# First projection in row halves with turned tiles between its chunks, and earlier requests for small inputs and for the second expert tile's weights

## What is computed

```python
n = rms_norm(h, norm1_g[l])                 # h is x, 1024 x 1024
proj = n @ w_in[l]
(q_att, c_kv, q_idx, k_idx, w_idx, r_q, r_k, r_v, r_gate, g_att, g_ret) = jnp.split(proj, points, axis=-1)
...                                         # sparse indexed attention, retention, gated merge, h = h + mixed @ w_out
n2 = rms_norm(h, norm2_g[l])
h = h + hierarchical_moe(n2, ...)           # top-1 group, top-2 of 16 experts, SwiGLU
```

## Time and profile before

| | us |
|---|---|
| median of the three runs | 1532.45 |
| the profiled execution | 1532.13 |
| its span | 1530.3 |
| PE busy in the span | 1447.9 |
| DVE busy | 1089.7 |
| ACT busy | 769.0 |
| POOL busy | 570.6 |
| mean granted TensorE clock | 0.973 |

### The profile page before, as it was taken

One profiled execution on the slowest core, in us unless ns is written; L12 is line 12 of the kernel. 1 busy time (PEld: TensorE's weight loads), 2 busy tenths in 40 slices (PEclk: granted clock), 3 DMA queues, 4 the chain that ended last, 5 costly groups with the idle time before them and its releaser, 6 DMA issues.

```text
span 1530.3 us, 19995 instructions
## 1 busy us (share of the span) xinstructions
PE 1447.9 (95%) x7190; PEld 1203.0 (79%) x7190; DVE 1089.7 (71%) x1518; ACT 769.0 (50%) x1270; POOL 570.6 (37%) x418
## 2 busy tenths in 40 slices
PE   5999999999999998899999999999999489999995
PEld 5987888987889887677667788888887478888884
DVE  4328999999999965776648943236533689999994
ACT  5237323236422526766533442223335378888884
POOL 2310221463424276100135543332232156775655
PEclk9998999999999998999999999999999599999998
DMA  5210121113221034111155334445325888899995
GB/s 193 63 35 1 35 49 42 42 35 110 79 53 42 22 115 167 56 56 28 42 192 192 98 125 143 148 147 174 148 83 185 286 278 253 272 241 354 271 292 75
DMA packets 93937, 199.91 MB, mean 131 GB/s; under 512 B 11664, under 2 KB 33424, under 8 KB 91536
## 3 DMA queue, kind: packets, MB, share of 16 engines
q1 hardware_dynamic: 76560, 158.01, 30.7%
q0 software_dynamic: 13392, 32.51, 9.7%
q10 hardware_dynamic: 3888, 8.13, 1.4%
HBM read 206.22 MB, written 39.58 MB: 161 GB/s over the span
## 4 chain that ended last, share of the span: by engine, by line
PE 74%; DMA 10%; DVE 6%; ACT 3%; issue 3%; POOL 2%; ACTq 0%; SPq 0%; DVEq 0%; POOLq 0%
PE ps L782 21%; PE ps L783 21%; PE ps L784 21%; DMA out<-e_y,dest 8%; PE ps L1011 4%; PE ps L1001 2%; DVE dist L1735 1%; DMA w_raw<-in_w_in 1%; PE ps L1144 1%; PE ps L949 1%; DMA xin<-in_x 1%; POOL out L2319 1%; PE ps L962 1%; DVE f_sum L1846 1%; DMA e_raw<-in_w_up 1%
## 5 line engine op out<-in xcount | busy, mean ns | idle before, releaser
L2178 POOL TENSOR_TENSOR w_lo<-w_raw,w_hi 128x512 fp32r<-128x512 f32 (+1 forms) x184 | 254.7, 1389 | 599.8 <-ACT w_hi L1219 523.4
L1219 ACT CAST w_hi<-w_raw 128x512 fp32r<-128x512 f32 (+1 forms) x184 | 111.8, 614 | 402.9 <-PE ps L784 352.2
L782 PE MATMUL ps<-w_hi,n_hi 128*128 128x512 f32 (+2 forms) x704 | 243.7, 346 | 1.8 <-ACT ro L1378 1.6
L784 PE MATMUL ps<-w_hi,n_lo 128*128 128x512 f32 (+2 forms) x704 | 242.0, 344 | 0.0
L783 PE MATMUL ps<-w_lo,n_hi 128*128 128x512 f32 (+2 forms) x704 | 241.9, 344 | 0.0
L2116 DVE TENSOR_TENSOR e_lo<-e_raw,e_hi 128x2048 fp32r<-128x2048 f32 x93 | 213.2, 2296 | 29.3 <-ACT e_hi L1610 28.8
L1610 ACT CAST e_hi<-e_raw 128x2048 fp32r<-128x2048 f32 x93 | 177.8, 1914 | 40.5 <-DMA e_raw<-in_w_up 24.1
L2319 POOL DMA_INDIRECT out<-e_y,dest x62 | 142.5, 2299 | 99.6 <-DMA out<-e_y,dest 72.2
L1774 DVE MAX8 small<-dist 128x8 f32<-128x384 f32 (+5 forms) x192 | 171.8, 895 | 6.6
L782 PE MATMUL ps<-n_hi,w_hi 128*128 128x512 f32 x416 | 164.3, 395 | 6.6 <-POOL w_lo L2178 2.6
L1775 DVE MATCH_REPLACE8 dist<-small,dist 128x384 f32<-128x384 f32 (+5 forms) x192 | 168.1, 875 | 0.0
(11 more groups left out here) (277 smaller groups left out, 2858.1 us busy)
## 6 DMA issues: line engine op xcount, KB each, us to landing
e_raw<-in_w_gate SPq DMA_DIRECT2D x64, 512.0 KB
e_raw<-in_w_up SPq DMA_DIRECT2D x64, 512.0 KB
e_raw<-in_w_down SPq DMA_DIRECT2D x32, 1024.0 KB
w_raw<-in_w_in SPq DMA_DIRECT2D x120, 256.0 KB, 2.7
a_raw<-att_dram SPq DMA_DIRECT2D x16, 512.0 KB, 3.4
a_raw<-ret_dram SPq DMA_DIRECT2D x16, 512.0 KB, 3.3
w_raw<-in_w_out SPq DMA_DIRECT2D x24, 256.0 KB, 3.4
w_raw<-in_w_in SPq DMA_DIRECT2D x40, 128.0 KB, 2.3
```

The costliest lines, as they stand in the source:

```text
L782: mm(out, a[0], b[0], start=first, stop=False, skip_group_check=skip)
L784: return mm(out, a[1], b[0], start=False, stop=last, skip_group_check=skip)
L1219: nc.scalar.copy(w_hi[c % NH][:, :width], split_from(c)[:, :width]).then_inc(hi_ready, 1)
L2178: G.tensor_tensor(w_lo[c % NH][:, :width], split_from(c)[:, :width], w_hi[c % NH][:, :width].bitcast(F32), ALU.subtract).then_inc(lo_ready, 1)
```

## The change

The first projection's first four row tiles are taken ahead of the others. PE turns the first four row tiles one by one as they are scaled; it then takes chunks 0 and 1 for row tiles 0 to 3, turns half of the other four tiles, takes chunk 2, turns the rest, takes chunk 3, takes chunks 0 to 3 for row tiles 4 to 7, and chunks 4 to 7 for all. The second half is turned into banks 4 to 7 alone. `hi(3)` goes ahead of `turned_hi(1)`, and `hi(0)` stands between the two halves of `turned_hi(0)`. 1/rms and the scaling go tile by tile, and the last row tile is squared on DVE. The identity and the gains are loaded behind the second row tile, the rest of `cst` and `w_up` behind the first four chunks; whoever reads them waits for `rest_in`. The residual's x tiles reuse the semaphores of the first x loads. SP no longer waits ahead of tile 1's expert weights.

```diff
-        for half in range(2):
-            for k in range(KT):
-                bk.use(("xT", half, k), k)
-        use_block("kv")
+        for k in range(KT):
+            bk.use(("xT", 0, k), k)
+        for b in range(4):
+            bk.use(("kv", b), b)
+        for k in range(KT):
+            bk.use(("xT", 1, k), 4 + k % 4)
+        for b in range(4, 8):
+            bk.use(("kv", b), b)
@@ SP
-                if t == 3:
-                    sp.dma_start(cst[:], w["cst"]).then_inc(const_in, 16)
+                if t == 1:
+                    sp.dma_start(cst[:, K_ID:K_REL], w["cst"][:, K_ID:K_REL]).then_inc(const_in, 16)
                     sp.dma_start(gains[:, 0:NGAIN], w["gains"]).then_inc(const_in, 16)
-            for j in range(2):
-                sp.dma_start(w_up[:, j, :], w["w_kv_up"][j * P:(j + 1) * P, :]).then_inc(up_in, 16)
             for c in range(ga + 4):
                 load_chunk(c)
+                if c == NR - 1:
+                    sp.dma_start(cst[:, K_REL:], w["cst"][:, K_REL:]).then_inc(rest_in, 16)
+                    for j in range(2):
+                        sp.dma_start(w_up[:, j, :], w["w_kv_up"][j * P:(j + 1) * P, :]).then_inc(up_in, 16)
...
-                if i.n == 1:
-                    sp.wait_ge(ex_in[1], 16)
@@ PE
-            for half in range(2):
-                pe.wait_ge(xn_done, 4 * (half + 1))
+            for t in range(4):
+                pe.wait_ge(xn_done, t + 1)
                 for k in range(KT):
-                    bk.wait_free(pe, ("xT", half, k))
+                    last = turn_x(0, k, t)
+                    if t == 3:
+                        bk.filled(last, ("xT", 0, k))
+            def turn_second(ks):
+                pe.wait_ge(xn_done, NT)
+                for k in ks:
+                    bk.wait_free(pe, ("xT", 1, k))
                     for t in range(4):
...
-            gemm("kv")
+            def kv_rows(k, tiles):
+                c = number["kv"] * KT + k
+                pe.wait_ge(lo_ready, c + 1)
+                for b in tiles:
+                    if k == 0:
+                        bk.wait_free(pe, ("kv", b))
+                    t = slice(b * P, (b + 1) * P)
+                    last = three(bank(("kv", b), KVW), (n_hi[:, k, t], n_lo[:, k, t]),
+                                 (w_hi[c % NH][:, :KVW], w_lo[c % NH][:, :KVW]), k == 0, k == KT - 1)
...
+            kv_rows(0, range(4))
+            kv_rows(1, range(4))
+            turn_second(range(0, 4))
+            kv_rows(2, range(4))
+            turn_second(range(4, KT))
+            kv_rows(3, range(4))
+            for k in range(4):
+                kv_rows(k, range(4, 8))
+            for k in range(4, KT):
+                kv_rows(k, range(8))
...
+            pe.wait_ge(rest_in, 16)        # ahead of the index products; ACT, DVE and POOL wait for it too
@@ ACT
-            square_x(range(NT))
+            square_x(SQ_ACT)               # SQ_ACT = range(NT - 1)
             act.wait_ge(const_in, 16 * 2)
-            turned_hi(0)
-            for c in range(NH - 1):
+            turned_hi(0, range(0, 4))
+            hi(0)
+            turned_hi(0, range(4, KT))
+            for c in range(1, NH):
                 hi(c)
             turned_hi(1)
@@ DVE
-            for pair in range(NT // 2):
-                dve.wait_ge(rstd1, pair + 1)
-                for t in range(2 * pair, 2 * pair + 2):
-                    V.tensor_scalar(xin[:, t, :], xin[:, t, :], small[:, 8 + t:9 + t], None, ALU.mult).then_inc(xn_done, 1)
+            def square_x(t):
+                dve.wait_ge(x_in[t], 16)
+                V.tensor_tensor_reduce(out=junk_v[:], in0=xin[:, t, :], in1=xin[:, t, :], scale=1.0, scalar=0.0,
+                                       op0=ALU.mult, op1=ALU.add, accum_out=small[:, t:t + 1]).then_inc(sq_dve, 1)
+            for t in range(5):
+                norm_x(t)                  # waits for rstd1 >= t + 1, then the same scaling of one tile
+            square_x(NT - 1)
             dve.wait_ge(const_in, 16 * 2)
+            turned_lo(0, range(0, 4))
+            for t in range(5, NT):
+                norm_x(t)
+            turned_lo(0, range(4, KT))
+            turned_lo(1)
...
-            turned_lo(0)
-            turned_lo(1)
@@ POOL
-            for pair in range(NT // 2):
-                pool.wait_ge(sq_done, 2 * (pair + 1))
-                rstd(small[:, 8 + 2 * pair:10 + 2 * pair], small[:, 2 * pair:2 * pair + 2], 2, D, (rstd1, 1))
+            for t in range(NT):
+                if t in SQ_ACT:
+                    pool.wait_ge(sq_done, SQ_ACT.index(t) + 1)
+                else:
+                    pool.wait_ge(sq_dve, 1)
+                rstd(small[:, 8 + t:9 + t], small[:, t:t + 1], 1, D, (rstd1, 1))
```

More of the change, by code:

```diff
@@ L265, in program @@
         junk = r1t("junk", [P, 2, D], 15488)
+        junk_v = r1t("junk_v", [P, D], 15488 + 2 * D)
         rqT = [r1t(f"rqT{i}", [P, S], i * S) for i in range(2)]
@@ L364, in program @@
         n2_dram = scratch["n2"]
-        const_in, up_in = sem("const_in"), sem("up_in")
+        const_in, rest_in, up_in = sem("const_in"), sem("rest_in"), sem("up_in")
         x_in = [sem(f"x_in{t}") for t in range(NT)]
@@ L373, in program @@
         s_dve, s_act, s_pool = sem("dve_seq"), sem("act_seq"), sem("pool_seq")
+        sq_dve = sem("sq_dve")
         sq_done, rstd1, xn_done, nhi_done = sem("sq_done"), sem("rstd1"), sem("xn_done"), sem("nhi_done")
@@ L393, in program @@
         mixed, mix_hi, mix_lo = sem("mixed"), sem("mix_hi"), sem("mix_lo")
-        xres_in, h_stored = [sem(f"xres_in{t}") for t in range(NT)], sem("h_stored")
+        h_stored = sem("h_stored")
         rt_in, h_half_sq, h_sq, h_rstd, n2_done, n2_stored = (sem(n) for n in ("rt_in", "h_half_sq", "h_sq", "h_rstd", "n2_done", "n2_stored"))
@@ L554, in program @@
             {"block": use_block, "phase1": use_phase1, "phase2": use_phase2, "turn": use_turn, "first": use_first}[what](n)
+        SQ_ACT = range(NT - 1)
         STEPS = NT * HA
@@ L716, in _ @@
                     for t in range(2 * k - 8, 2 * k - 6):
-                        sp.dma_start(xres[:, t, :], w["x"][t * P:(t + 1) * P, :]).then_inc(xres_in[t], 16)
+                        sp.dma_start(xres[:, t, :], w["x"][t * P:(t + 1) * P, :]).then_inc(x_in[t], 16)
             def load_weights(b, j, e, **new):
@@ L859, in _, with turn_x @@
             pe.wait_ge(const_in, 16 * 2)
-            for half in range(2):
-                pe.wait_ge(xn_done, 4 * (half + 1))
+            def turn_x(half, k, t):
+                return tr(bank(("xT", half, k))[:, t * P:(t + 1) * P], xin[:, 4 * half + t, k * P:(k + 1) * P], ident)
+            for t in range(4):
+                pe.wait_ge(xn_done, t + 1)
                 for k in range(KT):
-                    bk.wait_free(pe, ("xT", half, k))
-                    for t in range(4):
-                        last = tr(bank(("xT", half, k))[:, t * P:(t + 1) * P],
-                                  xin[:, 4 * half + t, k * P:(k + 1) * P], ident)
-                    bk.filled(last, ("xT", half, k))
-            gemm("kv")
+                    last = turn_x(0, k, t)
[5 more added lines that the diff above has]
+                    bk.wait_free(pe, ("xT", 1, k))
+                    for t in range(4):
+                        last = turn_x(1, k, t)
+                    bk.filled(last, ("xT", 1, k))
+            def kv_rows(k, tiles):
[7 more added lines that the diff above has]
+                                 (w_hi[c % NH][:, :KVW], w_lo[c % NH][:, :KVW]), k == 0, k == KT - 1)
+                    if k == KT - 1:
+                        bk.filled(last, ("kv", b))
+                    elif b == 7:
+                        last.then_inc(chunk_used, 1)
+            kv_rows(0, range(4))
[8 more added lines that the diff above has]
+                kv_rows(k, range(8))
             gemm("qi")
@@ L1223, in square_x, with turned_hi @@
                     act.wait_ge(x_in[t], 16)
[L1224 to L1229, removed]
+                    n = SQ_ACT.index(t)
+                    if n >= 2:
+                        act.wait_ge(sq_done, n - 1)
+                    A(junk[:, n % 2, :], xin[:, t, :], ACT.Square, accum_out=small[:, t:t + 1]).then_inc(sq_done, 1)
+            def turned_hi(half, ks=range(KT)):
+                for k in ks:
                     name = ("xT", half, k)
@@ L1243, in ahead @@
                     hi(number[name] * KT + k + NH - 1)
-            ahead("kv")
+            for c in range(NH, KT + NH - 1):
+                hi(c)
             for t in range(NT):
@@ L1254, in _ @@
             act.wait_ge(gains_done, 1)
+            act.wait_ge(rest_in, 16)
             for j in range(2):
@@ L1673, in _, with turned_lo @@
             V = nc.vector
-            def turned_lo(half):
-                for k in range(KT):
+            def turned_lo(half, ks=range(KT)):
+                for k in ks:
                     name = ("xT", half, k)
```

(21 more changed lines are left out.)

## The result

| | median us | lowest to highest, runs | ratio to before, 95% interval | profiled, us | its span |
|---|---|---|---|---|---|
| before | 1531.53 | 1529.22 to 1533.86, 6 | | 1532.13 | 1530.3 |
| changed | 1522.38 | 1519.90 to 1524.33, 6 | 0.9939 [0.9925, 0.9952] | 1520.5 | 1518.7 |
| changed, measured again (e10 below) | 1522.18 | 1520.53 to 1524.75, 6 | 0.9940 [0.9927, 0.9953] | 1524.75 | 1523.0 |

The kernel became 0.6% faster: 9.2 us between the medians, 9.3 [7.4, 11.5] by the ratio. 1524.0 had been forecast, in a range of 1519.5 to 1530.5.

A forecast was written before the change was run, and what follows sets the result against it. PE was taken to bound the kernel, with 74% of the chain of waits (DMA 10%). 1532.13 - 4.2 (head) - 4.2 (expert stage) = 1523.7, the median 0.3 higher: 1524.0 us, range 1519.5 to 1530.5.

The forecast's parts named there:

- Loads: Head: identity and gains ahead add 0.19 us; third row tile lands at 7.86, the last at 14.35 instead of 17.38.
- The square on DVE: Head: DVE squares the last row tile from 14.35, taken as 1.2 us, between 1.06 and 2.3.
- rival B: Head: the low clock lasts 10 us and DVE's square costs 2.3 us; 1527.2 us in total; chance 14%.
- Start and clock: Head: PE starts the projection at 18.2, low clock for 5.1 us, block "qi" at 53.4 instead of 57.63, gaining 4.2 us.
- Rival D: Head: PE never gets the high clock while turns and chunks alternate, so the kernel is slower, 1536.3 us; chance 4%.
- The value of the clock: Head: each further us of low clock costs 0.46 us; no low stretch at all would gain 6.5 us.
- Issue and landing of tile 1's weights: Expert stage: tile 1's loads start at 1208.5, the first part lands at 1218.7; PE's 4.6 us gap falls to 1.
- The expert term: Expert stage: the next result is turned at 1235.8 instead of 1239.97, gaining 4.2 us; bounds 2.7 and 5.2.
- Rival A: Expert stage: early weights only fill the queue or scatters absorb the gain, so it gives nothing; 1528.2 us; chance 17%.
- Gathers: Expert stage: earlier weights touch only the end of tile 0's gather, nothing charged; by the queue rule 4.0, not 4.2.
- Rival C: Expert stage: all 3 MB of weights go ahead of tile 0's rows, 2.6 us lost; 1530.8; 10% with both parts lost.
- The end: Last chain: the scatter-adds have caught up with PE, so the kernel's end moves with PE.

The follow-up runs named there:

- e10: The changed kernel itself without an edit, measured again: 1522.18 us, 0.9940.
- e1: The changed kernel with the wait ahead of tile 1's expert weights put back, so the head's part alone: 1524.00 us, 0.9950.
- e2: The kernel before with only the wait ahead of tile 1's expert weights taken out: 1526.39 us, 0.9967.
- e4: The changed kernel with the old order of loads and tile 1's wait put back, so the new order of work alone: 1527.87 us, 0.9975.
- e6: The changed kernel with the last row tile squared on ACT, as before the change, instead of DVE: 1523.74 us, 0.9953.
- e7: The changed kernel with PE repeating the first half's last transpose 28 times to shorten its idle stretch ahead of the projection: 1523.29 us, 0.9950.
- e3: The kernel before with the new loads, tile-by-tile 1/rms and scaling and DVE's square, but the old PE and ACT order and the wait: 1527.36 us, 0.9971.
- e5: The changed kernel with DVE squaring the last row tile behind its first four low parts instead of in front: 1525.02 us, 0.9957.
- e8: The changed kernel with chunk 0 loaded behind the fourth row tile and the work of ACT, POOL, DVE and PE reordered: 1520.43 us, 0.9933.
- e9: As e8, but POOL computes 1/rms of row tiles 6 and 7 as one pair: 1520.27 us, 0.9929.

## Why the prediction was right, point by point

- **Loads.** Third tile 7.86 and last 14.35 predicted; 7.89 and 14.31 measured. The distance between them, the rate, holds elsewhere too (8.49 and 14.91 in e1, 8.45 and 14.89 in e10). The exact hit of the first was a favourable draw: in the eight other profiles with these loads the third tile stands at 7.95 to 8.49, and the mean of the nine is 8.21. With the old loads it is 7.67, 7.38 (e2) and 7.40 (e4), mean 7.48. So the term for identity and gains ahead of the third tile, 0.19, is 0.7 between the means.
- **The square on DVE.** 1.2 was taken, out of 1.06 to 2.3; it is 1.23. The dear square of rival B is out, and e6 shows that the square is on the path when it stands in front of ACT's evictions.
- **Start and clock.** Start at 18.2 predicted, 18.03 measured, 18.44 in e1 and 18.61 in e10. Low for 5.1 us from there predicted; windows of 0.1 us put the return of the clock at 22.4 (4.4 us), 24.1 in e1 and 24.4 in e10 (5.7 and 5.8). In all three the granted clock was low for 6.8 us; it fell at 15.6, 17.3 and 17.6, inside the idle stretch. So 5.1 was a fair mean, and a single draw is 0.6 to 0.7 off. 0.27 a matmul instead of 0.28. Block "qi" at 53.4 predicted; 52.59, 53.56 (e1) and 53.46 (e10), mean 53.2, measured, against 57.63 and 57.23 (e2) for the old head, mean 57.4: 4.2 us, the predicted term. Rival D, a clock that never comes back, is out: it is 1.00 from 25 on in all three.
- **Small slips.** The old head's turns took 6.13 / 32 = 0.192 and 6.58 / 32 = 0.206 us each, not 0.205 in both halves, and low for 10 us gives 4.9 x 0.46 = 2.3 less, so 2.0 and not 2.1. Neither changes the forecast.
- **The value of the clock.** "Each further us of low clock costs 0.46" is the step that does not hold below the forecast: e7 took the low stretch away, and 0.86 us of it came back as a wait for POOL. It made the bound of 6.5 too high and left the sum alone.
- **Issue and landing of tile 1's weights.** Its first part 14.3 us behind the token predicted (1218.7 - 1204.43), 13.5 measured, 13.5 to 14.9 over the eight executions. Gap of PE 1 predicted, 0.93 measured, up to 1.42 in the eight.
- **The expert term.** 4.2 predicted, 4.8 between the two profiles (35.54 - 30.73), 3.5 between the means of four executions with the wait and eight without (33.76 - 30.30). The mechanism was right; that the size fits is in part luck. The reference was read off one execution whose gap, 4.67 us, is the longest of the four that keep the wait, and whose second turn is 1.8 us above their mean (35.54 against 33.76). The forecast turn, 1235.8 - 1204.43 = 31.4, is 1.1 above the mean of the eight: tile 2's weights were put on ACT 26.6 us behind the token and came at 24.4 to 25.8. The two errors nearly cancel. e2's median says 4.6 by itself. Rival A (early weights only fill the queue) is out: e2 alone gives 0.9967 [0.9956, 0.9979].
- **Gathers.** No delay was charged. Tile 0's rows reach PE 5.7 to 6.0 us behind the token in the four profiles with the wait and 5.6 to 6.2 in the eight without, in the mean 5.84 and 5.81. Rival C is out. The Trainium skill's rule of turns between queue rows (page "DMA: Bandwidth & Descriptors", section "Queues, rings and completion order"), by which tile 0's gather should lose a few tenths, is neither shown nor excluded by this: the spread is as large, and PE had no wait for a later tile's rows.
- **The end.** The last turn of a result moved from 1510.29 to 1498.52 and the last scatter from 1520.18 to 1508.53, 11.8 and 11.65: the end moves with PE, as said. The last scatter starts 9.9 to 10.1 us behind the last turn in eleven of the twelve profiles; in e10 it is 12.5, so 2.5 us of that slow execution were lost behind PE.
- **The sum.** 4.2 + 3.5 = 7.7 by positions, 9.3 [7.4, 11.5] by the ratio. Of the 11.6 between the first two profiles, 2.0 is the stretch with the wait at 793 us; in the other executions that wait is 0.28 to 1.37 or absent, as in e2, e3 and both of the changed kernel. The medians' 1.5 us beyond 7.7 lie inside the interval. The stretch from block "qi" to the token took 1144.8 to 1147.4 us over the twelve profiles, and both old heads (1146.8 and 1145.6) lie inside that: a spread wider than the missing 1.5 us. But e1, the head alone, is 6.9 [4.7, 10.7] us faster, where the positions count 4.2. Whether the head gains something that they do not show, the runs leave open.

## What to carry to other kernels

Before moving one operation, list what the engines have in program order behind whoever waits for its result: e5 freed DVE and blocked POOL. Count a stall's removal only up to the next engine that is late there, as e7 and e8 showed, where 0.86 and 1.43 us came back as other waits. And size a DMA wait from several executions, for the one that was profiled may hold the longest gap.

## What had not been expected of the hardware

The clock's fall was not a matter of the idle stretch's length alone. Behind 3.11 us of idle (e4) PE stayed at 2.4 GHz, and behind 1.84 us (e9) it went to 1.2 GHz. The windows of e4, of e9 and of the kernel before, the clock in the last column but two:

```profile
18.00:21.00 3.00, 0.12 (x1) 0.12 (x2) 3.00 (x7) 3.00 (x7) 2.34 (x4) 1.00 0.28 76
21.00:24.00 3.00, 2.20 (x13) 1.93 (x14) 3.00 (x5) 2.28 (x6) 1.37 (x2) 1.00 0.23 56
```

```profile
15.00:19.00 4.00, 3.75 (x16) 3.21 (x17) 4.00 (x7) 4.00 (x9) 2.84 (x3) 0.75 1.04 395
19.00:22.00 3.00, 3.00 (x17) 3.00 (x17) 3.00 (x5) 1.29 (x3) 2.09 (x4) 0.77 0.68 184
```

```profile
19.00:21.00 2.00, 0.00 (x0) 0.00 (x0) 1.39 (x3) 2.00 (x5) 0.58 (x1) 1.00 0.03 9
21.00:22.00 1.00, 0.00 (x0) 0.00 (x0) 0.97 (x5) 1.00 (x3) 0.00 (x0) 0.60 0.00 0
```

What PE did before the idle stretch differs: in e4 it had turned 32 blocks without a break (12.04 to 17.77), in e9 a row tile at a time, with gaps. And in e9 the fall came when PE was at work again: it resumed at 15.25, and the starts stand 0.27 us apart only behind 17.14. Neither explains all cases. The kernel before had also turned 32 blocks without a break (12.76 to 18.89), its stretch of 3.19 us was hardly longer than e4's, and its clock fell, between 21 and 22, with PE still idle. In e8, behind 1.44 us, the clock stayed high. What decides was not tried, so no length of idle time can be called safe from these runs.
